# A three-layer transformer kernel on one core: key and query lengths as logarithms, another order of the input tiles, and a first modulation split between two engines

## The reference, cut to what matters

```
m = silu(cond) @ w + b            # 6 * 1024 values: shift1, scale1, gate1, shift2, scale2, gate2
h = rms_norm(x, g) * (1 + scale1) + shift1
a_u, a_v, qkv, gate, alpha_raw, beta_raw = split(h @ w_in)
```

```
q, k, v = split(silu(dwconv(qkv)));  q = q * rsqrt(sum(q*q)+eps) / sqrt(128);  k = k * rsqrt(sum(k*k)+eps)
beta = sigmoid(beta_raw);  log_alpha = -exp(a_log) * softplus(alpha_raw + dt_bias)
gcum = cumsum(log_alpha);  decay_ij = exp(gcum_i - gcum_j) for j <= i
A = strictly_lower((k*beta) k^T * decay);  T = inverse(I + A)
u = T (v*beta);  w = T (k*beta*exp(gcum));  attn = (q k^T) * decay
scan over chunks: v_new = u - w s;  o = (q*exp(gcum)) s + attn v_new;  s = s*exp(g_end) + (k*exp(g_end-gcum))^T v_new
```

## Time and profile before

| | us |
|---|---|
| median of 3 runs (lowest, highest) | 1726.2 (1725.77, 1733.74) |
| the profiled execution's own time | 1728.06 |
| its span in the trace | 1725.8 |
| TensorE busy, mean granted clock | 1612.8, 0.957 |
| VectorE busy | 1124.1 |
| ScalarE busy | 790.8 |

### The profile page before, as it was taken

One profiled execution on the slowest core, in us unless ns is written; L12 is line 12 of the kernel. 1 busy time (PEld: TensorE's weight loads), 2 busy tenths in 40 slices (PEclk: granted clock), 3 DMA queues, 4 the chain that ended last, 5 costly groups with the idle time before them and its releaser, 6 DMA issues.

```text
span 1725.8 us, 31269 instructions
## 1 busy us (share of the span) xinstructions
PE 1612.8 (93%) x11526; PEld 1399.2 (81%) x11526; DVE 1124.1 (65%) x1893; ACT 790.8 (46%) x1426; POOL 111.0 (6%) x129
## 2 busy tenths in 40 slices
PE   7999978978989999999989999999999988999998
PEld 1687867878767777788878579999898767999998
DVE  0679465355469999976554547886566665577653
ACT  2545423223254444432245446776444445566532
POOL 1000033030100000001000010001100000000000
PEclk9999888789989999999989999999899999999999
DMA  9355300000135555555442114556454322355552
GB/s 354 119 177 190 133 26 9 1 2 2 61 99 186 187 181 186 183 183 172 134 154 86 49 51 146 184 191 208 160 177 152 99 86 73 123 161 186 189 183 97
DMA packets 62840, 230.47 MB, mean 134 GB/s; under 512 B 6752, under 2 KB 8032, under 8 KB 62240
## 3 DMA queue, kind: packets, MB, share of 16 engines
q1 hardware_dynamic: 61344, 223.37, 38.7%
q0 software_dynamic: 1120, 5.54, 0.9%
q10 hardware_dynamic: 288, 0.33, 0.1%
HBM read 228.17 MB, written 1.05 MB: 133 GB/s over the span
## 4 chain that ended last, share of the span: by engine, by line
PE 82%; DVE 10%; ACT 4%; issue 3%; DMA 1%; POOL 0%; DVEq 0%; ACTq 0%; SPq 0%; POOLq 0%
PE proj L628 21%; PE proj L630 20%; PE proj L629 20%; DVE w_low L2018 2%; PE bank L680 1%; DMA a_first<-a_head 1%; ACT w_high L1517 1%; PE proj L703 1%; PE bank L874 1%; PE bank L891 1%; PE bank L1159 1%; PE bank L894 1%; PE bank L726 1%; PE bank L1155 1%; PE bank L1110 1%
## 5 line engine op out<-in xcount | busy, mean ns | idle before, releaser
L628 PE MATMUL proj<-h_high,w_high 128*128 128x256 f32 (+1 forms) x1768 | 583.8, 330 | 21.1 <-DVE h_low L2051 12.3
L629 PE MATMUL proj<-h_low,w_high 128*128 128x256 f32 (+1 forms) x1768 | 571.9, 323 | 0.0
L630 PE MATMUL proj<-h_high,w_low 128*128 128x256 f32 (+1 forms) x1768 | 571.4, 323 | 0.0
L2018 DVE TENSOR_TENSOR w_low<-w_raw,w_high 128x1024 fp32r<-128x1024 f32 x322 | 393.2, 1224 | 207.7 <-ACT w_high L1517 206.5
L1517 ACT ACTIVATE w_high<-w_raw 128x1024 fp32r<-128x1024 f32 x322 | 337.9, 1054 | 236.9 <-PE proj L630 234.8
L628 PEld LDWEIGHTS proj<-h_high,w_high 128*128 128x128 f32 x1768 | 337.0, 191 | 65.0 <-issue 17.6
L630 PEld LDWEIGHTS proj<-h_high,w_low 128*128 128x128 f32 x1768 | 337.6, 191 | 27.4
L629 PEld LDWEIGHTS proj<-h_low,w_high 128*128 128x128 f32 x1768 | 337.1, 191 | 25.3
L630 PE MATMUL proj<-act_high,w_low 128*128 128x256 f32 (+1 forms) x608 | 189.8, 312 | 0.0
L628 PE MATMUL proj<-act_high,w_high 128*128 128x256 f32 (+1 forms) x608 | 189.5, 312 | 0.4 <-DVE w_low L2018 0.4
L629 PE MATMUL proj<-act_low,w_high 128*128 128x256 f32 (+1 forms) x608 | 189.5, 312 | 0.0
(11 more groups left out here) (403 smaller groups left out, 1957.3 us busy)
## 6 DMA issues: line engine op xcount, KB each, us to landing
w_raw<-w_stream SPq DMA_DIRECT2D x322, 512.0 KB, 3.9
a_ring<-a_stream SPq DMA_DIRECT2D x80, 512.0 KB, 3.9
a_first<-a_head SPq DMA_DIRECT2D x4, 2048.0 KB, 20.4
x<-x_in SPq DMA_DIRECT2D x1, 2048.0 KB, 13.5
late_tab<-late_tables POOLq DMA_DIRECT2D x1, 1408.0 KB, 6.6
cond_rows<-cond_rows SPq DMA_DIRECT2D x1, 1024.0 KB, 18.5
cond_rows<-cond_rows POOLq DMA_DIRECT2D x1, 1024.0 KB, 5.1
x<-mem_in POOLq DMA_DIRECT2D x1, 1024.0 KB, 6.0
```

Of the source, the lines that this page charges most:

```text
L628: mm(out_, wh, xh, start=first, stop=False)
L629: mm(out_, wh, xl, start=False, stop=False)
L630: return mm(out_, wl, xh, start=False, stop=last)
L2018: v.tensor_tensor(wl(n), RAW[:, n % 4, :], wh(n), ALU.subtract).then_inc(w_low, 1)
```

## The change

Five things are done together.

1. **Lengths as logarithms.** q and k are no longer multiplied by their inverse lengths. The logarithm of the sum of squares, times -1/2 (for q with log 128 added first), is added to or subtracted from the cumulated logarithms: `RP` for rows, `CP` for columns, and `BE`, `EK`, `BR`, `GE` are formed in one tensor `EX` and exponentiated in one instruction. `inverse_lengths`, `over_lengths`, the square root, the reciprocal and the copy of the end factors (L2261) are gone.
2. **Order of the tiles.** q, k, v become tiles 0 to 11, alpha and beta tile 12, the spatial gate's tiles 13 to 20, the output gate's stay 21 to 24. The sum of squares of tile t-4 stands behind tile t.
3. **The first stream's preparation beside the tiles.** Transposed gates behind tile 13, cumulative sums behind 14, key products behind 15 and 16, rows, decays, exponentials, triangles for q = 0 to 3 behind tiles 17, 19, 21, 23, all in one pair of banks. In both streams the decays no longer wait for the exponential of the same bank, which now comes second on ScalarE.
4. **Spatial products** go from steps 24 to 27 of the first stream to steps 4 to 7 of the second.
5. **First modulation.** Chunks 0 to 7 stay on TensorE, now with a stationary operand of 128 columns (two of them hold the condition, the rest is zero); chunks 8 to 15 are row blocks on VectorE. The condition rows load first, then x, then 1 MB issues of both kinds by turns.

```diff
+            for g in range(2):
                 for k in range(KC):
+                    if k % 4 == 0:
+                        pe.wait_ge(a_first[2 * g + k // 4], 16)
+                    if g == 1 and k == 4:
+                        norm_spread("n1_0")
+                    last = mm(MROWS[g][:], CW[:, k, :], A16[:, 4 * g + k // 2, k % 2 * 512:(k % 2 + 1) * 512], start=(k == 0), stop=(k == KC - 1))
...
+            for t in range(4, GATES):
                 tile(t, t, slice(0, T2), T2)
+                lengths(t - 4)
...
+            for t in range(GATES, 25):
+                tile(t, t, slice(0, T2), T2)
+                if t == 13:
                     pe.wait_ge(G["g_soft"], 1)
                     for x in range(4):
                         last = nc.tensor.transpose(BK[0][:, 40 * x:40 * x + 40], GT[0:40, x * P:(x + 1) * P], ID[0:40, 0:40])
                     last.then_inc(G["g_tr"], 1)
+                if t == 14:
+                    pe.wait_ge(G["g_tok"], 1)
+                    pe.wait_ge(gdn_in, 16)
...
+                if t == 15:
+                    pe.wait_ge(silu_done, 8)
+                    key_products(0, 0)
+                if t == 16:
+                    pe.wait_ge(G["g_cum"], 1)
+                    key_products(0, 1)
+                    pe.wait_ge(G["g_fac"], 1)
+                if t in ROWS_AT:
+                    rows(0, ROWS_AT[t])
```

On ScalarE (`f` is an activation):

```diff
+            for t in range(GATES):
+                split(t + 2)
+                conv_in(t, t, 0, COL_AT["bconv"], T2)
+                act.wait_ge(conv_done, t + 3)
+                f(QKV[:, t, :], C1[:, t % 2, :], ACT.Silu).then_inc(silu_done, 1)
+                if t < 8:
+                    act.wait_ge(silu_done, t + 1)
+                    f(squared(t), QKV[:, t, :], ACT.Square).then_inc(G["l2_sq"], 1)
...
+            def prelim_exp(st, q):
+                z = 4 * st + q
+                act.wait_ge(G["gb_d"], z + 1)
+                f(DT[:, z % 2, :, :], DT[:, z % 2, :, :], ACT.Exp).then_inc(G["gb_e"], 1)
+                if z >= 2:
+                    act.wait_ge(G["gb_q"], z - 1)
+                f(ER[:, z % 2, :, :], rows_banks(st, q)[0][:].rearrange("p (a b) -> p a b", a=HEADS), ACT.Exp).then_inc(G["gb_e"], 1)
```

On VectorE, the first modulation and the tiles from 12 on:

```diff
+            for m in range(A_FIRST - A_COLS):
+                if m % 2 == 0:
+                    dve.wait_ge(a_rows[m // 2], 16)
+                w = A16[:, A_COLS + m, :]
+                for s, o in enumerate((PROD0[:], w)):
+                    if m and s == 0:
+                        dve.wait_ge(m_front, 2 * m - 1)
+                    v.scalar_tensor_tensor(o, w, 1.0, CB0[:, s, :], ALU.mult, ALU.mult,
+                                           accum_out=MODF[:, 2 * (A_COLS + m) + s:2 * (A_COLS + m) + s + 1]).then_inc(m_front, 1)
...
+            for t in range(GATES, 24):
                 low(t + 2)
-                mod_tile(t, CB0, PROD0)
-                if t == 21:
+                if t == 13:
 
                     dve.wait_ge(G["g_in"], 1)
                     link(v.scalar_tensor_tensor(GA[0:8, :], GA[0:8, :], 0.0, GB[0:8, :], ALU.max, ALU.add))
                     v.tensor_scalar(GT[0:8, :], GA[0:8, :], SM[0:8, 4:5], -1.0, ALU.mult, ALU.mult).then_inc(G["g_soft"], 1)
...
+                if t == 14:
+                    dve.wait_ge(G["g_tr"], 1)
+                    v.tensor_copy(GTOK[:], BK[0][:, 0:160].rearrange("p (t r) -> p t r", t=4)).then_inc(G["g_tok"], 1)
...
+                if t in ROWS_AT:
+                    decays(0, ROWS_AT[t])
+                    triangles(0, ROWS_AT[t])
+                mod_tile(t, CB0, PROD0)
```

More of the change, by code:

```diff
@@ L366, in two_blocks_kernel @@
         GC = place("g_cum", [P, 4, 2, 8])
[L367 to L370, removed]
+        L2 = place("qk_lengths", [P, 4, 8])
+        LR = place("qk_log_factors", [P, 4, 8])
+        RP = place("log_rows", [P, 4, 2, HEADS])
+        CP = place("log_cols", [P, 4, 2, HEADS])
+        EX = place("factors", [P, 4, 4, 2, HEADS])
+        BE, EK, BR, GE = (EX[:, i, :, :, :] for i in range(4))
         inverse_at = cursor[0]
@@ L725, in lengths @@
                 for t in range(4):
-                    last = mm(BK[0][:, 8 * t + j:8 * t + j + 1], SQL[:, j % 4, t * P:(t + 1) * P], ONES[:, 0:1], start=True, stop=True)
+                    last = mm(BK[4][:, 8 * t + j:8 * t + j + 1], squared(j)[:, t * P:(t + 1) * P], ONES[:, 0:1], start=True, stop=True)
                 last.then_inc(G["l2_ss"], 1)
[L729 to L736, removed]
@@ L739, in _, with rows @@
-            for t in range(20, 25):
-                tile(t, t, slice(0, T2), T2)
-                if t in (20, 21):
-                    for j in range(4 * (t - 20), 4 * (t - 20) + 4):
-                        lengths(j)
-                if t == 23:
-                    pe.wait_ge(G["l2_std"], 1)
-                    inverse_lengths(range(4))
+            for t in range(4, GATES):
+                tile(t, t, slice(0, T2), T2)
+                lengths(t - 4)
+            def rows(st, q):
+                tl, d, z = q // 2, q % 2, 4 * st + q
+                tt = 2 * st + tl
+                if st == 0 and q:
+                    pe.wait_ge(G["gb_at"], z)
+                    pe.wait_ge(G["gb_e"], 2 * z)
+                elif q >= 2:
+                    pe.wait_ge(G["gb_at"], z - 1)
+                    pe.wait_ge(G["gb_e"], 2 * z - 2)
+                sums, betas = rows_banks(st, q)
+                for h in range(HEADS):
+                    mm(sums[:, h * P:(h + 1) * P], RP[:, tt, d, h:h + 1].to_broadcast([P, P]), ID[:], start=True, stop=True)
+                    last = mm(betas[:, h * P:(h + 1) * P], BR[:, tt, d, h:h + 1].to_broadcast([P, P]), ID[:], start=True, stop=True)
+                last.then_inc(G["gb_r"], 1)
@@ new lines, in key_products @@
+            def key_products(st, tl):
+                tok = slice(st * SEQ + tl * P, st * SEQ + (tl + 1) * P)
+                for h in range(HEADS):
+                    mm(bank(2 + 2 * tl, 4, P)[:, h, :], QKV[:, 4 + h, tok], QKV[:, 4 + h, tok], start=True, stop=True)
+                    last = mm(bank(3 + 2 * tl, 4, P)[:, h, :], QKV[:, 4 + h, tok], QKV[:, h, tok], start=True, stop=True)
+                last.then_inc(G["gb_k"], 1)
+            for t in range(GATES, 25):
+                tile(t, t, slice(0, T2), T2)
+                if t == 13:
@@ L1608, in _ @@
             norm_root("n1_0")
-            for g in range(4):
-                if g == 3:
+            for g in range(2):
+                if g == 1:
                     split(0)
@@ L2139, in _ @@
             dve.wait_ge(cond_ready, 2)
-            with dve.Fori(0, 2) as i:
+            with dve.Fori(0, 3) as i:
                 for s in range(4):
                     low(s + 2, 4 * i)
+                    conv(s, s, 0, COL_AT["bconv"], T2, i, 4)
                     mod_tile(s, CB0, PROD0, 4 * i)
-            with dve.Fori(0, 3) as i:
-                for s in range(4):
-                    low(8 + s + 2, 4 * i)
-                    conv(8 + s, s, 0, COL_AT["bconv"], T2, i, 4)
-                    mod_tile(8 + s, CB0, PROD0, 4 * i)
```

348 lines of the change are left out of this document (172 added, 176 removed).

## The result

The changed kernel takes 1709.0 us (median of four runs, 1705.1 to 1709.4) against 1727.6 for the kernel before on the same chip: a ratio of 0.988, 95% interval 0.987 to 0.990. Forecast were 1701 and a range of 1687 to 1717. The profiled execution took 1709.05 (span 1707.2), 18.6 us of span less than before, where the sum said 25.1.

The account below looks back on a forecast made before the run. TensorE was taken as the bound, with 82% of the chain. Shifts of -20.8 (front and tiles included), -1.5, -1.9 and -0.9 sum to -25.1 us: 1703 for the profiled execution, 1701 as median, range 1687 to 1717.

Parts of the forecast that it names:

- Front: Loads, first modulation and first norm: first projection matmul at 43.5 us, 7.6 us earlier, bounds 5 and 10.
- Tiles: The 25 input tiles: 23.1 us leave, 19.1 of work and 13.3 of waits come in, 174.0 us long, 9.3 longer.
- The waits: TensorE idle behind tiles 13, 14 and 16: 7.2, 2.7 and 1.0 us; with low clock 13.3 together, bounds 5 and 20.
- wait (a): Behind tile 13 TensorE waits for the gates' softplus, 7.2 us idle, reckoned without a drain at table loads.
- From tile 24 to the levels: Level step 0 starts 4.5 us after tile 24, bounds 2 and 9; step 3 ends 20.8 us earlier, front and tiles included.
- Spatial products: Moved from the first stream's last four steps to the second's steps 4 to 7: -13.5 plus 12, net -1.5 us.
- Second stream's preparation: Decays no longer wait for the same bank's exponential and four small copies go: -1.9 us, range 0 to -3.5.
- two GpSimd products: They leave the first stream's steps: -0.9 us.
- A: Rival: short sums and rows between tiles repeatedly take TensorE's clock down; +40 us, 1741, slower; chance 5%.
- B: Rival: VectorE or ScalarE bounds the tiles and late low parts stall TensorE; 1.5 us on ten tiles, 1716; chance 14%.
- D: Rival: preparation only moves from idle into busy TensorE time and waits eat the rest; some 1722, no difference; chance 4%.
- C: Rival: waits at tiles 13 and 14 half as long, spatial products at high clock; -6 and -6, 1689; chance 14%.

Follow-up runs that it names:

- experiment 7: Changed kernel with the first norm's squares summed on TensorE instead of GpSimd, no new tile, and VectorE's reciprocal behind the seventh row block: 1705.0 us, ratio 0.988.
- Experiment 2: Changed kernel with seven unused matmuls before the gates' transposes at tile 13 and three before the cumulative sums at tile 14: 1701.3 us, ratio 0.984.
- experiment 3: Changed kernel with only the spatial products moved back to steps 24 to 27 of the first stream: 1712.5 us, ratio 0.991.
- experiment 1: Changed kernel with gates' transposes and cumulative sums one tile later and VectorE's gate work ahead of the low part: 1690.0 us, ratio 0.978; repeated, 1689.9.
- experiment 4: Changed kernel with only the old front back, all 16 groups of the first modulation on TensorE and the earlier transfer order: 1710.3 us, ratio 0.989.

## Why the prediction was right, and what it missed

Direction, size and mechanism came out: the preparation leaves the path between tile 24 and the levels, part of it comes back as TensorE work in the tiles. That the total lies so near is in part luck: steps that were 2 to 3 us off, in both directions, partly made each other good. Step by step:

- **Front, -7.6 forecast, -4.8 measured.** Here the prediction failed in a price: "VectorE takes one row block for both streams in 2.3 us", eight of them ending at 36.6; they ended at 40.6, because the earlier trace rows were taken where GpSimd is idle, and here it adds squares from 16.6 to 26.7. (The 36.6 is also a slip: 17.4 + 8 x 2.3 + 0.2 is 36.0, and in experiment 7, without the additions, they ended at 36.0.) The Trainium skill (SBUF — State Buffer, Who interferes with whom) says that a VectorE instruction with both inputs in SBUF and a GpSimd instruction that reads SBUF exclude each other for their whole length. The rows agree: 2.27 against 1.22 us, and GpSimd's five additions 10.09 against 6.9 in the kernel before. TensorE's half was 2 us late too (41.9 for 39.7), though its weights had landed at 32.3 (32.7 forecast): it had stood 3.32 us for GpSimd's additions, which took 3.2 longer than before. An estimate from these rows is that TensorE's half would be through some 3 us earlier without the contention; experiment 7, which put longer sums in the additions' place, gave 0.6 and doesn't decide it.
- **Tiles, 174.0 forecast, 176.3 measured.** The waits were 6.75, 2.70 and 0.88 for 7.2, 2.7 and 1.0. The term left out is the clock behind the second wait: the cumulative sums and tile 15 ran low too, some 2.5 us. Experiment 2 gives 4.8 for the low clock in all, where I had put 2.4 behind the first wait and nothing behind the second. The wait (a) came out without a drain behind the table loads, as the row said; the Trainium skill's 1.38 us a switch (ScalarE: Activation LUTs, What ACT_TABLE_LOAD costs) did not show.
- **From tile 24 to the levels, 4.5 forecast, 4.47 measured.** The whole lack of 5.2 at level step 3 is that of the two steps above (2.8 and 2.3).
- **Spatial products, -1.5 forecast; -4.8 between the two profiles (-15.9, +1.3, +8.5, +1.3), -5.7 by experiment 3 up to the second stream's output sums.** The forecast's 13.5 out started from 21.7 us, a stretch that begins at the first spatial product (294.8); step 24 begins at 291.9, and the four steps took 25.1. They now take 9.2, where I took 8.2. The steps 4 to 7 of the second stream ran at the high clock after the first of them, 8.5 where I took 12. The first 1.3 is the u/w products of the first stream, which stay low for longer; the other lies between the second stream's two sets of output sums. This made good 3 us.
- **Second stream's preparation, -1.9 forecast, -2.2 measured.** (The terms named there, 1.18, 0.65 and four times 0.15, add up to 2.4.)
- **What no step held:** 3.1 us at 1295 us. 21 matmuls of an untouched stage took 6.85 us at clock 0.51; in experiment 1 the same took 3.74:

```profile
1280.00:1283.74 3.74, 3.74 (x21) 3.09 (x21) 1.48 (x3) 1.05 (x3) 0.00 (x0) 1.00 0.26 79
```

The sum of -25.1 lacks 2.8 and 2.3, wins 3.3 and 0.3, lacks the 0.9 that two GpSimd products were to give (no row shows it) and these 3.1: -19.6, against -18.9 at the third norm from the end. "What follows the second stream's level steps is untouched, so the sum is a sum of shifts" was the sentence that did not hold to 3 us.

The rivals: A (the clock taken down by sums between tiles) is refuted by 1.00 over the tiles with sums; the rule cited for it, that a little busy array slows, did not show behind the sums, and in the tiles only behind the two stands of 6.75 and 2.70 us. It did show elsewhere without a stand: in the earlier trace rows and in experiment 3 the steps with the spatial products kept TensorE busy nearly throughout, at 0.53 and 0.59. B did not happen, conv tiles show no wait, nor did D, whose 1722 was not reached. C had its half about the spatial products nearly right (three of the four steps ran high), and the waits wrong.

## What to carry to other kernels

Price a new wait of the bound engine as the wait plus the clock behind it, here a third of the whole (4.8 of 14.7 us); and look whether its result is needed there at all, since meeting the same chain one tile later, with VectorE's part of it put first, cost nothing and was worth 14.7 us in its stage, where the whole change had given 18.6. A duration taken from a row holds for the company it was measured in: before moving an operation, look at what VectorE's neighbour GpSimd does at the new place. And a few us won ahead of a stretch with many small waits may be given back there by the clock (4.8 became 1.8 in experiment 4). Compare stretches only from the same piece of work to the same piece of work.

## What was not expected of the hardware

- A VectorE pass over 128x1024 with both inputs in SBUF took 2.27 us beside GpSimd's additions and 1.22 without, while the rate of the transfers was the same.
- 32 bytes more in front of TensorE's moving operands stretched the spacing of 128x512 matmuls from 229.1 to 233.4 ns and the kernel by 9 us; 64 bytes gave 232.9 and 6 us. The cause is open.
- The same 21 matmuls ran at either clock level from kernel to kernel (6.85 or 3.74 us), and the first stream's levels took 55.8, 57.7, 58.7 or 60.7 us, with the same instructions in each or nearly so.
